# The attention loop's key product moves to the bank of the values' product

## The reference

```
kv = (kv_c @ w_ukv).reshape(bsz, n, N_HEADS, QK_NOPE + V_DIM)        # 12 heads, 64 + 64
s = einsum('bqhd,bkhd->bhqk', qn, k_nope) + einsum('bqhr,bkr->bhqk', qp, k_pe)
p = softmax(s * scale)
o = einsum('bhqk,bkhd->bqhd', p, v)
```

## Time and profile before

| | us |
|---|---|
| median of 3 runs | 806.44 |
| lowest, highest | 806.28, 810.97 |
| profiled execution, device time | 812.16 |
| its span in the profile | 810.3 |
| PE busy | 707.8 (87%) |
| DVE busy | 233.7 (29%) |
| POOL busy | 177.6 (22%) |
| ACT busy | 140.5 (17%) |
| DMA, mean | 264 GB/s |

### The profile page before, as it was taken

One profiled execution on the slowest core, in us unless ns is written; L12 is line 12 of the kernel. 1 busy time (PEld: TensorE's weight loads), 2 busy tenths in 40 slices (PEclk: granted clock), 3 DMA queues, 4 the chain that ended last, 5 costly groups with the idle time before them and its releaser, 6 DMA issues.

```text
span 810.3 us, 9735 instructions
## 1 busy us (share of the span) xinstructions
PE 707.8 (87%) x3677; PEld 397.1 (49%) x3678; DVE 233.7 (29%) x485; ACT 140.5 (17%) x288; POOL 177.6 (22%) x232
## 2 busy tenths in 40 slices
PE   2788999999989997899989898798799899999940
PEld 0334444554555654466344553455445556666620
DVE  1200212222162232122340423355221722322315
ACT  2201000001211121121130211345111121221201
POOL 4000111110421222122130100465314122222203
PEclk9899999999988999899999999899799889999975
DMA  9999798493074999988684512904200859979934
GB/s 340 391 344 354 294 361 334 182 407 140 26 296 136 420 422 420 420 347 338 250 351 169 214 47 99 421 7 153 101 33 27 311 187 416 377 273 420 420 146 170
DMA packets 52620, 213.97 MB, mean 264 GB/s; under 512 B 13985, under 2 KB 21153, under 8 KB 33393
## 3 DMA queue, kind: packets, MB, share of 16 engines
q1 hardware_dynamic: 31520, 178.59, 55.3%
q0 software_dynamic: 10240, 24.38, 8.4%
q10 hardware_dynamic: 10832, 10.63, 4.1%
HBM read 207.57 MB, written 15.43 MB: 275 GB/s over the span
## 4 chain that ended last, share of the span: by engine, by line
PE 68%; DMA 18%; DVE 6%; issue 3%; ACT 2%; POOL 1%; SPq 1%; ACTq 0%; POOLq 0%; DVEq 0%
PE ps L1304 14%; PE ps L1235 11%; PE ps L1329 7%; DMA pool<-in_mod_w 7%; PE ps L1378 7%; DMA pool<-in_moe_w 6%; PE ps L1422 5%; PE ps L1172 4%; PE ps L1539 3%; PE ps L1395 3%; PE ps L1467 2%; PE ps L1288 2%; DMA pool<-y_rows 2%; PE ps L1225 2%; PE ps L1521 1%
## 5 line engine op out<-in xcount | busy, mean ns | idle before, releaser
L1304 PE MATMUL ps<-pool 128*64 128x256 f32 x1280 | 146.9, 388 | 8.7 <-issue 6.7
L1304 PEld LDWEIGHTS ps<-pool 128*64 128x64 f32 x1280 | 106.6, 140 | 53.6 <-issue 21.3
L1235 PE MATMUL ps<-pool,yT 128*128 128x512 f32 x192 | 86.5, 606 | 0.0
L1329 PE MATMUL ps<-pool 128*64 128x512 f32 x320 | 73.1, 597 | 4.6 <-DMA pool<-in_moe_w 2.1
L1172 PE MATMUL ps<-pool,cs 128*32 128x512 f32 x384 | 49.3, 645 | 24.0 <-DMA pool<-in_mod_w 13.7
L1378 PE MATMUL ps<-hT,pool 128*128 128x384 f32 x192 | 65.6, 496 | 0.0
L1235 PEld LDWEIGHTS ps<-pool,yT 128*128 128x128 f32 x192 | 36.4, 194 | 42.4 <-issue 42.2
L534 POOL TENSOR_SCALAR pool<-pool 128x384 f32<-128x384 f32 (+1 forms) x36 | 36.5, 1029 | 77.2 <-DVE pool L1102 77.1
L1378 PEld LDWEIGHTS ps<-hT,pool 128*128 128x128 f32 x192 | 37.2, 198 | 31.5 <-issue 10.3
L932 DVE SCALAR_TENSOR_TENSOR pool<-ps,pool 128x256 f32<-128x256 f32 x20 | 9.7, 484 | 128.8 <-PE ps L1304 128.8
L1329 PEld LDWEIGHTS ps<-pool 128*64 128x64 f32 x320 | 25.0, 136 | 38.9 <-issue 37.4
(11 more groups left out here) (220 smaller groups left out, 785.5 us busy)
## 6 DMA issues: line engine op xcount, KB each, us to landing
pool<-in_moe_w SPq DMA_DIRECT2D x96, 1024.0 KB, 13.3
pool<-in_mod_w SPq DMA_DIRECT2D x24, 2048.0 KB, 11.1
pool<-in_ev_w_in SPq DMA_DIRECT2D x6, 1024.0 KB, 20.6
pool<-in_ev_w_in SPq DMA_DIRECT2D x2, 2048.0 KB, 24.3
ga<-mods POOLq DMA_DIRECT2D x8, 512.0 KB, 6.8
pool<-in_ev_w_out SPq DMA_DIRECT2D x2, 2048.0 KB, 10.6
pool<-mods POOLq DMA_DIRECT2D x8, 512.0 KB, 8.7
pool<-in_od_w_out SPq DMA_DIRECT2D x2, 2048.0 KB, 10.1
```

Of the source, the lines that this page charges most:

```text
L1235: ins = mm(ps[:, 2 * t + n, :], yT[:, k, t * P:(t + 1) * P], weight(parts[k // 4], 4, D)[:, k % 4, n * 512:n * 512 + 512], start=k == 0, s ...
L1304: ins = mm(ps[m, k, 0:DE], hTe.rearrange("p (c n) -> p c n", c=DC)[:, cc, m], w[e][:, cc, :], start=cc == 0, stop=cc == DC - 1)
L1329: ins = mm(ps[m, 4 + n, :], hidT[:, cc, m], w2[e][:, cc, n * 512:n * 512 + 512], start=cc == 0, stop=cc == 1)
```

## The change

`k_pair` writes bank 1 and ACT reads its keys there. The waits follow. `head_q` no longer waits for the key copy. `k_pair(g)` no longer waits for a query copy; from g = 3 on it waits until DVE has copied out the values of pair g-3, the last ones written to bank 1 before it. `pair_values(g)` gets a wait for the key copy of pair g+2 (or the last one), the last keys written to bank 1 before it. No instruction is added, dropped or moved in any engine's order.

```diff
@@ ACT, k_pair(g)
                 act.wait_ge(S("k_mm"), g + 1)
                 for b in range(2):
-                    ins = a_.activation(kT[0:NOPE, b, :], ps[b * NOPE:(b + 1) * NOPE, 0, :], ACT.Copy)
+                    ins = a_.activation(kT[0:NOPE, b, :], ps[b * NOPE:(b + 1) * NOPE, 1, :], ACT.Copy)
                 ins.then_inc(S("kT"), 1)
@@ PE, pair_values(g)
                 if g:
                     pe.wait_ge(S("o_out"), g)
+                pe.wait_ge(S("kT"), min(g + 3, NH // 2))
                 for kt in range(4):
@@ PE, k_pair(g)
-                if g:
-                    pe.wait_ge(S("qT"), 2 * g)
+                if g > 2:
+                    pe.wait_ge(S("o_out"), g - 2)
                 for cc in range(2):
                     for b in range(2):
-                        ins = mm(ps[b * NOPE:(b + 1) * NOPE, 0, :], ukv[:, cc, 2 * g + b, 0:NOPE], kvT[:, cc, :],
+                        ins = mm(ps[b * NOPE:(b + 1) * NOPE, 1, :], ukv[:, cc, 2 * g + b, 0:NOPE], kvT[:, cc, :],
                                  start=cc == 0, stop=cc == 1)
@@ PE, head_q(h)
                 if h:
                     pe.wait_ge(S("qT"), h)
-                pe.wait_ge(S("kT"), h // 2 + 1)
                 for t in range(TILES):
```

## The result

Against the kernel before on the same chip (four runs each) the changed kernel took a median of 796.72 us (795.75 to 800.68) and that one 807.95 us (806.28 to 810.97): a ratio of 0.9866, with a 95% interval from 0.9818 to 0.9915. That is 1.3% faster. The forecast was 801.3 us with a range from 798.7 to 806.0, a ratio of 0.9937 to the 806.44 us then known.

A forecast was written before the change was run, and what follows sets the result against it. PE's work plus two gaps in series, key copy and query copy, was taken to pace each pair. Gains of 1.25 + 1.24 + 2.60 = 5.09 us took the median from 806.44 to 801.3 us, range 798.7 to 806.0.

The forecast's parts named there:

- The closed gaps: PE's waits for the key copy before query transposes, removed in pairs 0 to 5: 1.25 + 1.24 + 2.60 = 5.09 us.
- Pairs 2 to 5: Query transposes run straight behind the probability transposes: 0.65 us gained at each of four places, lower end 0.47.
- Pair 0: Scores released by the key copy, moving from 498.52 to 497.27 us: a gain of 1.25 us.
- Pair 1: Same shape as the first pair; scores move from 515.41 to 514.17 us: a gain of 1.24 us.
- hand-over from ACT to PE: Time from the end of ACT's key copy until PE starts what waits for it: 0.14 us.
- The parts priced at nothing: k_pair's dropped query-copy wait and the new waits in k_pair and pair_values: worth or cost nothing.
- What stands behind: Everything after the closed gaps, through output projection and experts, follows in PE's order; no further gain or loss added.
- Rival 1: With shorter rests the clock may not fall after pair 1: 2.26 us more, median 799.1; chance 0.15.
- The main case: Closed gaps alone, nothing from the clock: median 801.3 us, span 800.9 to 802.4; chance 0.62.
- Rival 2: Low-clock stretches added elsewhere, up to 3.4 us each: one makes 804.7 us (chance 0.08), two 808.1 (0.03).

The follow-up runs named there:

- e1: Changed kernel with head_q waiting for the key copy again, key product still in bank 1; 804.87 us against 804.76 for the kernel before, ratio 1.0005.
- e2: Changed kernel with the key-copy wait kept for heads above 2, so only pairs 0 and 1 lose it; 799.35 us, 0.9943 of the kernel before.
- e6: Kernel before with products nobody reads filling the rests at the loop's end, no wait changed; 802.75 us, 0.9951 of the kernel before.
- e3: Changed kernel with the key-copy wait kept for heads 0 to 3, so only pairs 2 to 5 lose it; 802.90 us, 0.9976 of the kernel before.
- e9: Changed kernel with query transposes of head h+2 put ahead of the probability transposes of h-1 at even heads; 794.37 us, 0.9866 of the kernel before.
- e4: Kernel before with products nobody reads filling the rests of pairs 0 and 1, no wait changed; 802.74 us, 0.9978 of the kernel before.
- r4: Kernel before with the rests of pairs 0 and 1 filled by products nobody reads, a second time; 803.11 us, 0.9981 of the kernel before.

## Why the prediction was too small

**The closed gaps were right, place by place.** Pairs 2 to 5: 0.65 us each foreseen, 0.65 measured. Pair 0: 1.25 foreseen, 1.33 from key product to scores. Pair 1: 1.24 foreseen, 1.34. The 0.14 us that I added for a hand-over from ACT to PE was 0.04 where the scores waited for it, which is the difference. Sum 5.2 us against 5.09.

**The parts priced at nothing cost nothing.** No key product of pairs 3 to 5 shows a wait for the values copy, and e1, with both new waits in place, ran like the kernel before within its 0.3%.

**The step that failed is "What stands behind": that all else follows in PE's order, which takes it that the rest keeps its length.** The sum of 5.09 us holds the closed gaps alone and puts the clock behind them at nothing. Rival 1 had the mechanism and its price in the first turn, 2.26 us; the profile shows 2.16, and e2 a surplus of the same size over 12 runs (5.3 us against 2.6 of closed gaps, error 0.9). I gave it 0.15, arguing that the faster runs of before might never have had the fall. Some don't, as e6's profile shows for the same code, but the kernel before pays for it on the mean: filling its rests gained 2.5 us over 24 runs, 2.1 by the chips of those runs. The main case should have carried it. Rival 1's 799.1 us is 0.9909 of 806.44, beside 0.9902 for the pooled means, 797.63 to 805.51.

**The clock at the loop's end was not in the sum either.** Rival 2 looked only at falls that the change might add. The profile had one after the last heads [573 to 584 us above], and the change shortened it. In the kernel before, filling those rests gained 2.4 us by the means (4.1 by the runs beside it); in the changed kernel 0.7 with an error of 0.8, so nothing that shows. The waits there are the same ones in both kernels. Whether the changed one pays less for them, and why, stays open: it reaches them 7.4 us earlier after its pair 0 in the two profiles (67.18 us and not 74.57), and in the profiles with an unfilled end that fall came in three lengths: 10.2 us (the kernel before and e1), 3.4 us (the changed kernel three times, e3 and e9), and none (e2, e4 and r4, with rests of 1.91, 1.80 and 0.70 us like those before). That the moment decides is argued from these, not shown.

**Where the base stood.** The forecast was a difference taken from three runs. Of the 11.2 us between the medians of the first comparison, the closed gaps are 5.2, the clock about 2.7 (what is left of 7.9), and the other 3.3 luck of four runs or their chip. Over 98 runs the kernel before lies at 804.76 us (median), and the changed one over 22 at 797.36. The forecast difference of 5.1 us meets 7.9 with an error of 0.65; the ratios of the single comparisons were 0.8 to 1.3% below one.

**The spread goes with the clock.** In those 98 runs the mean granted clock of a run and its time go together with a correlation of -0.87: 19 runs below 0.9435 average 810.4 us, 29 runs between 0.9535 and 0.9575 average 802.9. At the same clock (0.9495 to 0.9535) the two kernels average 804.4 and 798.1 us, 6.4 apart; between 0.9535 and 0.9575 they average 802.9 and 796.5, 6.4 again.

**Transposes in the gap.** In these runs the clock in the first turn stayed up with the gap closed by transposes and with it filled by products alike, but closing it also moved the scores forward, so no run here separates the two. The Trainium skill, TensorE: Matmul & The Clock Gate, Part 4: PE-mode transpose, says that transposes don't count as activity in the way products do. By that rule the transposes moved into the gap would do nothing for the clock, and it would be the earlier scores; the runs neither bear this out nor speak against it.

## What to carry to other kernels

When a wait on PE is removed, count the gap, and then look at the granted clock in the microseconds behind it: if a stretch at the lower level follows the rest, what it costs belongs to the price, weighed by how often the stretch comes, for which one profile isn't enough. Then look for the next rest of the same kind further on; here the fall behind it changed too.

Where two steps share a PSUM bank only because one was free, the wait that guards it can put two copies in series. Ask of every wait whether it is for the data or for the bank, and once it is gone, whether an order that it forced can be turned too: that was worth another 3 us here (3.3, error 0.6).

## What the runs showed of the hardware

Where PE rested 1.3 to 1.4 us and, after three transposes, another 0.7 to 0.8 us, once in pair 0 and once in pair 1, three of four profiles show a stretch at the lower clock level of 1.2 GHz behind one of the two: 6.8 us (the kernel before, e1) or 3.4 us (e3). In the long one three score products took 3.33 us and not 1.75. Rests of 0.5 and 0.7 us every 10.7 us, in seven profiles, had no such stretch between them. Longer rests weren't always followed by one: 1.91, 1.80 and 0.70 us at the loop's end were in the kernel before, and were not in e2, e4 and r4. In the profiles with products of no use in the rests of pairs 0 and 1 the clock stayed at 1.00 there, the time was 2.5 us less by the means of 24 runs, and the products added 0.01 us (16.89 against 16.88 us from pair 0 to pair 1).

Runs of one and the same program spread over 14 us (798.71 to 812.89), and in the kernel before that goes with the mean granted clock of the run (correlation -0.87). Four runs a side were not enough to size a change of 1% here: the first comparison read 11 us, and 22 runs against 98 read 7.9.
